# Weight pieces, modulation steps and softmax scaling in the windowed attention of a two-layer trunk

## The reference

```python
def softmax_with_sink(s, sink):
    mx = jnp.maximum(jnp.max(s, axis=-1, keepdims=True), sk)
    e = jnp.exp(s - mx)
    return e / (jnp.sum(e, axis=-1, keepdims=True) + jnp.exp(sk - mx))

def attend_band(q, k, v, kc, vc, sink):      # |i-j| <= 128, plus 128 cached keys
    s_band = jnp.where(valid, s_band, -jnp.inf)
    p = softmax_with_sink(jnp.concatenate([s_band, s_ctx], axis=-1), sink)
    o = p[..., :nband] @ vband + p[..., nband:] @ vc

mod = jax.nn.silu(c) @ w_mod[l] + b_mod[l]   # w_mod[l]: (1024, 3072); shift, scale, gate
```

## Time and profile before

| | us |
|---|---|
| median of 3 runs | 1553.38 (1553.29 to 1554.37) |
| profiled execution, its own time | 1553.07 |
| its span | 1550.4 |
| TensorE busy | 1513.6 (98%) |
| VectorE busy | 733.6 (47%) |
| GpSimd busy | 642.9 (41%) |
| ScalarE busy | 464.3 (30%) |

### The profile page before, as it was taken

How to read it: one execution, slowest core, us unless ns; L and a number is a source line. 1 busy time by engine, 2 the same in 40 slices (tenths; PEclk the granted TensorE clock), 3 DMA queues, 4 the chain that set the end, 5 groups by cost and what they waited for, 6 DMA issues and landing times.

```text
span 1550.4 us, 22424 instructions
## 1 busy us (share of the span) xinstructions
PE 1513.6 (98%) x8995; PEld 1247.3 (80%) x8995; DVE 733.6 (47%) x1403; ACT 464.3 (30%) x1035; POOL 642.9 (41%) x573
## 2 busy tenths in 40 slices
PE   8999999999999999999999999999999999999997
PEld 6798788886788887788878977889768888778886
DVE  5596710646423333722497584126571136262257
ACT  1246710145410123411144485012661003232010
POOL 3551045711245453145773400556114554423562
PEclk9999999999999999999999999999999999999999
DMA  9420022327222222025431100222311221211421
GB/s 338 116 72 29 1 62 75 100 68 243 74 70 78 68 68 62 28 76 183 121 128 41 52 21 15 68 82 82 103 39 55 82 82 55 69 48 50 168 82 68
DMA packets 80486, 128.69 MB, mean 83 GB/s; under 512 B 16444, under 2 KB 29184, under 8 KB 80384
## 3 DMA queue, kind: packets, MB, share of 16 engines
q1 hardware_dynamic: 78144, 122.03, 24.8%
q10 hardware_dynamic: 2240, 5.24, 0.9%
HBM read 120.96 MB, written 6.30 MB: 82 GB/s over the span
## 4 chain that ended last, share of the span: by engine, by line
PE 82%; DVE 8%; POOL 3%; issue 2%; ACT 2%; DMA 2%; SPq 1%; POOLq 0%; DVEq 0%; ACTq 0%
PE pb L1067 55%; PE pb L1212 5%; PE pb L1336 4%; PE pb L1092 3%; PE pb L1287 3%; PE pb L1255 2%; PE pb L1011 1%; PE pb L1262 1%; PE pb L1517 1%; DMA raw<-in_w_in 1%; PE pb L1380 1%; DVE ks L2183 1%; POOL slot_T L890 1%; POOL wsp L890 1%; DMA stage<-in_w_mod 1%
## 5 line engine op out<-in xcount | busy, mean ns | idle before, releaser
L1067 PE MATMUL pb<-wsp,act_T 128*128 128x512 f32 x3048 | 713.3, 391 | 4.0 <-DVE act_T L2122 2.1
L1067 PEld LDWEIGHTS pb<-wsp,act_T 128*128 128x128 f32 x3048 | 568.1, 188 | 128.4 <-issue 7.1
L884 POOL CAST wsp<-raw 128x1024 fp32r<-128x1024 f32 x128 | 136.6, 1067 | 657.0 <-PE pb L1067 588.8
L890 POOL TENSOR_TENSOR wsp<-raw,wsp 128x512 fp32r<-128x512 f32 x268 | 360.3, 1365 | 9.9
L1067 PE MATMUL pb<-wsp,yT 128*128 128x512 f32 x720 | 165.7, 389 | 0.0
L1067 PEld LDWEIGHTS pb<-wsp,yT 128*128 128x128 f32 x720 | 135.0, 188 | 27.9
L2646 DVE SCALAR_TENSOR_TENSOR mt<-tg,pb 128x512 f32<-128x512 f32 x40 | 27.4, 685 | 216.6 <-PE pb L1067 215.8
L1948 ACT ACTIVATE tg<-pb 128x512 f32<-128x512 f32 x60 | 35.9, 599 | 275.9 <-PE pb L1067 275.9
L1287 PE MATMUL pb<-ident,pr 128*128 128x128 f32 x480 | 73.3, 273 | 2.7 <-ACT pT L1829 2.4
L2345 DVE TENSOR_SCALAR pr<-pr,rden 128x640 f32<-128x640 f32 (+2 forms) x128 | 70.4, 550 | 4.5
L2646 DVE SCALAR_TENSOR_TENSOR merged<-tg,pb 128x512 f32<-128x512 f32 x20 | 13.7, 687 | 119.9 <-PE pb L1067 119.9
(11 more groups left out here) (303 smaller groups left out, 1987.7 us busy)
## 6 DMA issues: line engine op xcount, KB each, us to landing
raw<-in_w_in SPq DMA_DIRECT2D x112, 512.0 KB, 3.5
raw<-in_w_mod SPq DMA_DIRECT2D x32, 512.0 KB, 4.5
raw<-in_w_branch SPq DMA_DIRECT2D x24, 512.0 KB, 3.6
raw<-in_w_out SPq DMA_DIRECT2D x16, 512.0 KB, 3.7
stage<-in_w_mod SPq DMA_DIRECT2D x28, 256.0 KB, 7.4
raw<-in_w_in SPq DMA_DIRECT2D x16, 256.0 KB, 5.1
xh<-in_x_sample SPq DMA_DIRECT2D x6, 512.0 KB, 6.0
out<-xh ACTq DMA_DIRECT2D x5, 512.0 KB, 2.9
```

The costliest lines, as they stand in the source:

```text
L884: pool.tensor_copy(hi, raw[:, p % 3, :, 0:width]).then_inc(raw_hi, 1)
L890: ins = pool.tensor_tensor(lo[:, j, :], raw[:, p % 3, j, 0:width], hi[:, j, :].bitcast(F32), ALU.subtract)
L1067: mm = pe.matmul(dst, lhs(a, k, t), w[:, wa, j, 0:width], start=(k == 0 and n == 0), stop=(i == count - 1 and j == 1 and n == 2))
```

## The change

Four edits. In the list of pieces, both G0 and G1 now stand ahead of all of the `w_mod` pieces of branch C; in layer 0, SyncE's stores of branch C's context keys go with them. `MOD_AT` of layer 0 is another set of 24 steps: 1, 3 to 14, and then 12 spread up to 28 with steps 15, 19 and 23 left out (before: 2 to 7 and 10 to 27); layer 1's table stays. GpSimd writes four sink columns, splits G0 and G1 one behind the other, and then writes the rest; `COLUMNS_SPLIT` is gone. VectorE scales unit s - 2 at step s in branch C, behind the maximum of unit s; the reciprocals of units q and q + 1 (q even) are one instruction on two columns, ahead of the scaling of q, and wait for the exponential of q + 1. Branch A keeps its order.

```diff
--- before.py
+++ after.py
@@ -188,8 +188,7 @@
 
 LATE_CHUNKS = (((1, 0), (1, 2), (1, 1), (1, 3), (0, 4), (0, 5)), ((1, 4), (1, 5)))
 
-MOD_AT = ((*range(2, 8), *range(10, 28)), (2, 4, 6, 8, 10, 12, 14, 16))
-COLUMNS_SPLIT = ((6, 11), (9, 18))
+MOD_AT = ((1, *range(3, 15), 16, 17, 18, 20, 21, 22, 24, 25, 26, 27, 28), (2, 4, 6, 8, 10, 12, 14, 16))
 OUT_SLOTS = (("A1", "A2", "M1", "M2"), ("Y1", "Y2", "w0", "w1"))
 KV_SLOTS = ("T1", "T2", "A1", "A2")
 Q_SLOTS = ("M1", "M2", "w0", "w1")
@@ -304,12 +303,9 @@
             if br == "C":
 
 
-                for n, (ll, c) in enumerate(LATE_CHUNKS[l]):
-                    if n == 1:
-                        add((br, "G", 0), "in", KD, (COL_G + BRANCH[br] * D, HALF), part=(0,))
+                add((br, "G", 0), "in", KD, (COL_G + BRANCH[br] * D, HALF), part=(0, 1))
+                for ll, c in LATE_CHUNKS[l]:
                     add(("gmod", ll, c), "mod", KD, (c * HALF, HALF), of=ll)
-                    if n == 1:
-                        add((br, "G", 0), "in", KD, (COL_G + BRANCH[br] * D, HALF), part=(1,))
             for s in range(STEPS[br]):
                 if s < NL:
                     psum.take((br, "S", s), *((2 * (s % 2), 2 * (s % 2) + 1) if br == "A" else (s % 3,)))
@@ -872,7 +868,7 @@
                         wait_full(pool, ("C", "PT", s - 4))
                     pool.tensor_copy(probs("C", s)[:, n:n + 1], sink[:, 1, h:h + 1]).then_inc(sink_column[l], 1)
 
-            def split(p, between=()):
+            def split(p):
                 nonlocal copies
                 width = sum(w for _, w in pieces.items[p][3])
                 wait_piece(pool, p)
@@ -882,24 +878,18 @@
                 else:
                     copies += 1
                     pool.tensor_copy(hi, raw[:, p % 3, :, 0:width]).then_inc(raw_hi, 1)
-                    sink_columns(here[0], between[0:1])
                     pool.wait_ge(raw_hi, copies)
                 for j in range(2):
-                    if j:
-                        sink_columns(here[0], between[1:2])
                     ins = pool.tensor_tensor(lo[:, j, :], raw[:, p % 3, j, 0:width], hi[:, j, :].bitcast(F32), ALU.subtract)
                 ins.then_inc(raw_used, 1)
 
             def branch_c(l):
 
-                g = pieces.at[l, ("C", "G", 0)]
-                a, b = COLUMNS_SPLIT[l]
                 edge_rows(l)
-                sink_columns(l, range(a))
-                split(g[0], (a, a + 1))
-                sink_columns(l, range(a + 2, b))
-                split(g[1], (b, b + 1))
-                sink_columns(l, range(b + 2, NL))
+                sink_columns(l, range(4))
+                for p in pieces.at[l, ("C", "G", 0)][0:2]:
+                    split(p)
+                sink_columns(l, range(4, NL))
 
             def splits(l, first, last):
 
@@ -2337,10 +2327,12 @@
                         n = len(key_blocks(br, t)) * P
                         o = slice(s % 4, s % 4 + 1)
                         if br == "C":
-                            dve.wait_ge(exp_done, l * NL + s + 1)
+                            if s % 2 == 0:
+                                dve.wait_ge(exp_done, l * NL + s + 2)
+                                step(dve.reciprocal(rden[:, s % 4:s % 4 + 2], lsum[:, s % 4:s % 4 + 2]))
                         else:
                             wait_done(dve, (br, "S", s))
-                        step(dve.reciprocal(rden[:, o], lsum[:, o]))
+                            step(dve.reciprocal(rden[:, o], lsum[:, o]))
                         p = probs(br, s)[:, 0:n]
                         dve.tensor_scalar(p, p, rden[:, o], None, ALU.mult).then_inc(p_ready[l], 1)
 
@@ -2396,8 +2388,9 @@
                             maximum(s)
                         if br == "C":
                             late_step(s)
-                        if 1 <= s < NL + 1:
-                            normalise(s - 1)
+                        lag = 1 if br == "A" else 2
+                        if 0 <= s - lag < NL:
+                            normalise(s - lag)
                         if s == NL:
                             maximum_context()
                         if s == NL + PV_AFTER[br] + 1:
```

## The result

The change makes the kernel slower: 1559.39 us median of 5 runs against 1553.38, ratio 1.0038 with a 95% interval of 1.0027 to 1.0049. The forecast was 1559.4. The profiled execution took 1559.39 too (span 1557.6, granted clock 0.998), 6.3 us above the one of before by its own time and 7.2 by its span: the one of before took 2.67 us more than its span, this one 1.8.

A forecast was written before the change was run, and what follows sets the result against it. TensorE was taken to bound the kernel (82% of the chain). Layer 0: 1.1 + 2.4 + 2.1 - 4.4 = +1.2; layer 1: 1.1 + 6.9 + 0.4 - 3.6 = +4.8; together +6.0, so 1559.4 us; 8-in-10 range 1554.5 to 1564.

The forecast's parts named there:

- The first scaling: Start of branch C's steps: first transposes wait for unit 0's scaling, held by unit 1's exponential; 1.1 us slower per layer.
- the hold of 0.2 that was kept for the upper end: First scalings beside G1's split: may be held 0 to 0.4 us per layer, counted only in the range's upper end.
- The scaling behind the next maximum: Odd steps without modulation: TensorE waits 0.53 us per pair of steps; 6.9 us layer 1 (13 pairs), 2.1 layer 0 (4).
- two copies: Layer 1, steps 9 and 17: a modulation row's copy on VectorE comes in between, 0.2 us each, 0.4 in all.
- the seven old waits for ScalarE in layer 1: TensorE's waits for copies of transposes; 3.6 us to go, as the same transposes would wait longer for VectorE.
- The ring: Layer 0's modulation pieces: all 4.4 us of mid-step waits go; late first pieces M1 and M2 cost 2.4 us.
- its list of what would show it wrong: Layer 1's steps at 56 us or under, no wait for the scaling, or waits for modulation pieces past step 5.
- the lower of the two landings: M2's piece in layer 0: landing 4.0 us after issue rather than 4.7, making the M1 and M2 term 2.0.
- The first: Rival: the ring and the freed VectorE decide, transposes find their scaling done; faster, 1550.1 us; chance 0.08.
- The second: Rival: new waits cover each other, one pair in two finds its scaling ready; no change, 1554.9 us; chance 0.11.
- The third: Rival: waits feed themselves through late copies, sink columns and maxima, 0.3 us more per pair; 1564.5 us; chance 0.12.
- The fourth: Rival: layer 0's waits for pieces are bandwidth, not the splits, and 4.4 us stay; 1563.8 us; chance 0.04.

The follow-up runs named there:

- The last experiment: The changed kernel with unit 0 alone scaled one step behind and single reciprocals for units 0 and 1; 1560.23 us, ratio 1.0036.
- the first experiment: The changed kernel with branch C's scaling back one step behind the maximum and one reciprocal a unit; 1552.12 us, ratio 0.9988 to the kernel before.
- the fourth experiment: The changed kernel with scaling one step behind, single reciprocals, and G0 and G1 behind all modulation pieces, splits behind the last sink column; 1547.89 us, ratio 0.9964.

## Why the prediction was right

**The first scaling.** Forecast 1.1 per layer. P0 started 1.29 late in layer 0 (340.67 against 339.38), by the hold of 0.2 that was kept for the upper end, and waited 1.16 in layer 1. The forecast named the exponential of unit 1 as what it waits for; in layer 0 after the change the reciprocal starts right behind the third maximum (339.69 and 339.71), so both end together there. The last experiment adds what the term left out: it is not P0's own. Behind it stand the pieces of M1 and M2 in layer 0 and unit 1's scaling in layer 1, so without it nothing comes back in layer 0 and 0.5 us in layer 1.

**The scaling behind the next maximum.** Forecast: 13 pairs at 0.53 and 0.4 for two copies, 7.3 us in layer 1. The page has 14 waits with P0, 6.4 listed; without P0's 1.16 that is 5.2, and with the 0.17 that each has ahead of the modelled end 13 × 0.17 = 2.2 more: 7.4. The two longest, 0.60, are the ones with the copy of a modulation row. In layer 0 four transposes wait (P13, P17, P21 and P27, as forecast: 0.21, 0.66, 0.33, 0.52; with 0.17 each 2.4 us against 2.1). One premise was not right: the seven old waits for ScalarE in layer 1 did not all stand at the transposes that now wait (P2 and P18 have even units). They are gone all the same. The runs show the mechanism from four sides: the scaling one step behind takes the waits away, modulation in odd steps hides them, fewer steps without modulation mean fewer waits, and a reciprocal more in front makes each longer.

**The ring.** Forecast: -4.4, and +2.4 for M1 and M2. M2 began at 344.44 where 342.77 (P0 at 340.67, and 2.10) would have been possible: 1.67, of which 0.27 was lost at M1. Two later pieces were waited for (0.17 at M6, 351.54, and 0.53 at M11, 362.98). The forecast ruled them out, and waits past step 5 stood in its list of what would show it wrong: that sign came. The step that failed is that pieces come in time once no split stands in the ring; it was read from the second half of the old table, and the new one has twelve modulation steps in a row. The sum, 2.37, is right, its make-up was not, and that it agrees is luck. M2's piece took 4.0 us from its issue at 340.42, the lower of the two landings. The Trainium skill (DMA: Bandwidth & Descriptors, "Latency and other measured facts") had the lower landing for a piece that is issued with little under way; the trace agrees for this one. It does not for M1's: that was issued at 336.83, after 16 us with a DMA share of 0.00, and M1 started 4.5 us later, in the first experiment 5.2 (336.86 to 342.03) and in the last 4.8. What makes it slower was not traced. The 16 us in the changed kernel (the last two values are the DMA share and GB/s):

```profile
320.00:336.00 16.00, 16.00 (x118) 15.97 (x117) 2.65 (x4) 5.80 (x8) 2.77 (x3) 1.00 0.00 0
```

**Sum.** Layer 0: 1.29 + 2.4 + 2.37 - 4.4 = +1.7, measured +1.73. Layer 1: 1.3 + 7.4 - 3.6 = +5.1, measured +5.43. In each layer one more old wait of 0.4 us went, for ScalarE's last copies, at the products with the values (L1336); it is in neither sum, and with it some 0.5 us in layer 0 and 0.8 in layer 1 were not traced. The forecast total of 6.0 stands against 7.16 in the steps, so the terms were short by 1.2 us, within the range. That the forecast 1559.4 and the measured 1559.39 agree is luck: the sum was added to an own time that lay 2.67 us above its span, where most executions of either kernel lie 1.8 above.

**The rivals.** The first wanted scalings that are done when TensorE comes, and TensorE waited for 13 pairs of 13. What it built on is real: with the scaling one step behind, the freed holds gave layer 1 0.7 us, where it had 1.3. The second wanted half of the pairs free, and none was. The third wanted lengthening waits, but those of layer 1 repeat (0.33, 0.26, 0.60, 0.46, 0.33, 0.33, 0.60, 0.45). The fourth fell with the fourth experiment as the cause of the 4.4: the same pieces in the same steps have 0.6 us of waits with G0 and G1 last. A small part of it is real: M6 and M11 wait with no split among the pieces, 0.7 us in the changed kernel and 1.3 in the first experiment.

## What to carry to other kernels

Software pipelining one step further back only helps if the delayed instruction does not at the same time move behind the newest step's work on an in-order engine: here the scaling of an old unit, long ready, stood behind a maximum that waited for TensorE's latest scores, and so TensorE waited for itself. Compare, step by step, what the engine behind has to do between two hand-overs with what the engine in front has; means over the stretch (VectorE 0.83 busy) did not show it here. Buffers of a shared ring that are held by a slow consumer belong behind the quick ones, and last in the queue if their own user comes last: the version with G0 and G1 last, the new table and the scaling as before takes 1547.9 us, 5.9 us under the kernel before. The old table with this ring was not run.

## What was not expected of the hardware

**Short instructions of VectorE last as long as GpSimd's.** The context's maximum has instructions on 8 columns that took 1.09 to 1.22 us beside a split and 0.17 behind it. The Trainium skill (SBUF — State Buffer, "Who interferes with whom") has this for an instruction with both inputs in SBUF: it is kept out while a GpSimd instruction reads there. The trace agrees for these: the one at 403.02 runs to 404.24, and the last split of that kernel to 404.22 (401.72 and 2.50). So the shorter the instruction, the worse the factor, here 7.

**TensorE's clock falls in a kernel that is 98% busy.** Behind a wait of 2.02 us in the first experiment and of 1.65 us in the last, the granted clock was 0.50 for 2 us and back at 1.00 some 2 us later. Each took about 1.6 us of TensorE's work, but little of the time, since TensorE would have had to wait for the next pieces (nothing is left of it at M5 in the first experiment, and 0.2 us at M2 in the last). The length of the wait alone does not decide it: behind the wait of 2.62 us with G0 and G1 last and the scaling late the clock stayed at 1.00, and with the old table in the changed kernel it fell behind waits of 1.16 and 0.75. The Trainium skill (TensorE: Matmul & The Clock Gate, Part 1) has the array's clock lowered when the engine is idle; what the traces add is that it can be lowered by one wait for a single late transfer. It also fell at 56 us in three of the profiled executions, behind a wait of 1.03 us that the changed kernel has too, with the clock at 1.00 behind it; there nothing behind it took the loss up, and they came 1.6 us later to branch C, besides what their waits in front were longer. That may be why medians of kernels whose steps differ by 1 us do not always stand in that order. With single reciprocals it fell at 22 us, behind a wait of 1.10 us, and that execution came to branch C no later than the others.
